# A two-block transformer kernel: seven more constant products at the start, and a final norm that is split over three engines and written out in four transfers

## The reference

```
proj = h @ w_in                       # first product: h is the input with the meta tokens
...
x = x + 0.5 * g3[:, None, :] * swiglu(h, w_gate, w_up, w_down)     # last down-projection
y = x * rsqrt(mean(x * x, axis=-1, keepdims=True) + 1e-6)          # final RMS norm
out = y * final_norm                                               # one weight per channel
```

## Time and profile before

| what | before |
|---|---|
| median of 3 runs | 1286.96 us (1286.91 to 1288.22) |
| profiled execution, its own time | 1286.66 us |
| its span, first to last instruction | 1284.7 us |
| TensorE busy | 1255.6 us, 98% |
| VectorE busy | 994.9 us, 77% |
| ScalarE busy | 685.4 us, 53% |
| GpSimd busy | 54.7 us, 4% |
| DMA, mean over the span | 191 GB/s |
| last chain by engine | TensorE 79%, VectorE 3%, ScalarE 1% |

### The profile page before, as it was taken

How to read it: one execution, slowest core, us unless ns; L and a number is a source line. 1 busy time by engine, 2 the same in 40 slices (tenths; PEclk the granted TensorE clock), 3 DMA queues, 4 the chain that set the end, 5 groups by cost and what they waited for, 6 DMA issues and landing times.

```text
span 1284.7 us, 29083 instructions
## 1 busy us (share of the span) xinstructions
PE 1255.6 (98%) x10579; PEld 1208.9 (94%) x10579; DVE 994.9 (77%) x1818; ACT 685.4 (53%) x1117; POOL 54.7 (4%) x93
## 2 busy tenths in 40 slices
PE   9999999999999999999999999999999999999997
PEld 8998898999999999999998899998899999999986
DVE  6897749998878898998877787775566768877654
ACT  6866445655543544665554565554365566655541
POOL 0012000000001000000000000000000000000000
PEclk9999999999999999999999999999999999999999
DMA  7541123688888588388875366665455336666651
GB/s 270 155 125 35 52 83 116 224 292 269 289 284 287 190 301 285 115 309 270 280 249 169 99 204 186 183 199 192 136 173 189 119 112 183 195 180 184 225 179 34
DMA packets 64778, 244.74 MB, mean 191 GB/s; under 512 B 7200, under 2 KB 8512, under 8 KB 64704
## 3 DMA queue, kind: packets, MB, share of 16 engines
q1 hardware_dynamic: 54048, 204.77, 48.8%
q0 software_dynamic: 10656, 38.93, 9.7%
HBM read 242.63 MB, written 1.05 MB: 190 GB/s over the span
## 4 chain that ended last, share of the span: by engine, by line
PE 79%; DVE 3%; ACT 1%; issue 1%; DVEq 0%; ACTq 0%
PE ps L1805 18%; PE ps L1804 18%; PE ps L1806 18%; PE ps L2170 10%; PE ps L2171 5%; PE ps L1819 1%; PE ps L1825 1%; PE ps L1820 1%; PE ps L2315 1%; PE ps L2317 1%; PE ps L2316 1%; DVE wlo L415 1%; PE ps L2426 1%; PE ps L2220 0%; DVE xb L1447 0%
## 5 line engine op out<-in xcount | busy, mean ns | idle before, releaser
L1804 PE MATMUL ps<-hhi,whi 128*128 128x258 f32 (+4 forms) x1952 | 557.4, 286 | 2.7 <-DVE hlo L1052 1.6
L408 ACT ACTIVATE whi<-raw 128x1024 fp32r<-128x1024 f32 (+1 forms) x360 | 400.3, 1113 | 292.7 <-PE ps L1806 169.9
L1805 PE MATMUL ps<-hlo,whi 128*128 128x258 f32 (+4 forms) x1952 | 555.5, 285 | 0.0
L1806 PE MATMUL ps<-hhi,wlo 128*128 128x258 f32 (+4 forms) x1952 | 550.1, 282 | 0.0
L415 DVE TENSOR_TENSOR wlo<-raw,whi 128x1024 fp32r<-128x1024 f32 (+1 forms) x360 | 463.5, 1293 | 86.4 <-ACT whi L408 81.8
L1804 PEld LDWEIGHTS ps<-hhi,whi 128*128 128x128 f32 x1952 | 369.9, 190 | 5.2 <-DVE wlo L415 4.2
L1806 PEld LDWEIGHTS ps<-hhi,wlo 128*128 128x128 f32 x1952 | 371.3, 190 | 0.0
L1805 PEld LDWEIGHTS ps<-hlo,whi 128*128 128x128 f32 x1952 | 369.9, 189 | 0.3
L2170 PE MATMUL ps<-aboth,whi 128*128 128x512 f32 x528 | 185.3, 395 | 0.0
L2171 PE MATMUL ps<-aboth,wlo 128*128 128x256 f32 x528 | 147.9, 280 | 0.0
L2170 PEld LDWEIGHTS ps<-aboth,whi 128*128 128x128 f32 x528 | 99.1, 188 | 22.9
(11 more groups left out here) (419 smaller groups left out, 1554.0 us busy)
## 6 DMA issues: line engine op xcount, KB each, us to landing
raw<-in_w_up SPq DMA_DIRECT2D x176, 512.0 KB, 4.1
raw<-in_w_down SPq DMA_DIRECT2D x64, 704.0 KB, 4.2
ring<-in_ada_w POOLq DMA_DIRECT2D x72, 512.0 KB, 5.0
raw<-in_w_mix SPq DMA_DIRECT2D x48, 512.0 KB, 3.5
raw<-in_w_a_in SPq DMA_DIRECT2D x32, 512.0 KB, 3.6
raw<-in_w_b_cx SPq DMA_DIRECT2D x16, 512.0 KB, 4.9
raw<-in_w_a_out SPq DMA_DIRECT2D x8, 512.0 KB, 3.6
raw<-in_w_b_gate SPq DMA_DIRECT2D x8, 512.0 KB, 4.4
```

The costliest lines, as they stand in the source:

```text
L408: nc.scalar.activation(whi[:, s, 0:blocks * P], raw[:, s, 0:blocks * P], ACT.Copy).then_inc(hi_split, 1)
L1804: nc.tensor.matmul(out, whi[:, s, w], rhi(k0 + k), start=first and k == 0, stop=False)
L1805: nc.tensor.matmul(out, whi[:, s, w], rlo(k0 + k), start=False, stop=False)
L1806: ins = nc.tensor.matmul(out, wlo[:, s, w], rhi(k0 + k), start=False, stop=last and k == blocks - 1)
```

## The change

Two things, in two places.

1. `WARM_UP` goes from 10 to 17: seven more products of the zeroed tile before the first unit.
2. The last norm. In `down3` ScalarE, after the square of tile m, multiplies `hf[:, m]` in place by the tile's column of weights. VectorE's products then need no column and are 512 wide (two tiles of `hf` by the row, which is read twice with a stride of zero); it makes three of them, tiles 0 to 5. TensorE writes the row a second time, to bank 6; ScalarE copies it to `tb`; GpSimd multiplies tiles 6 and 7 by that copy. SP writes out pairs of tiles, 256 KB each, in the order 0, 2, 6, 4.

```
-WARM_UP = 10
+WARM_UP = 17
...
-            for m in range(KT):
-                sp.wait_ge(y_ready, Y_AT[7] + m + 1)
-                sp.dma_start(io["out"][:, m, :], outb[:, m, :]).then_inc(out_done, 16)
-            sp.wait_ge(out_done, 16 * KT)
+            for i, m in enumerate((0, 2, 6, 4)):
+                if m == 6:
+                    sp.wait_ge(pool_out, 1)
+                else:
+                    sp.wait_ge(y_ready, Y_AT[7] + m // 2 + 1)
+                sp.dma_start(io["out"][:, m:m + 2, :], outb[:, m:m + 2, :]).then_inc(out_done, 16)
+            sp.wait_ge(out_done, 16 * (KT // 2))
...
+            pool.wait_ge(hg_ready, KT)
+            pool.wait_ge(row_copied, 1)
+            nc.gpsimd.tensor_tensor(outb[:, 6:8, :], hf[:, 6:8, 0:SEQ], bcast(tb[:, 0, 0:SEQ], 2), ALU.mult).then_inc(pool_out, 1)
...
                         nc.scalar.activation(sqb[:, m, 0:SEQ], hf[:, m, 0:SEQ], ACT.Square).then_inc(sq_ready, 1)
+                        if name == "down3":
+                            nc.scalar.activation(hf[:, m, 0:SEQ], hf[:, m, 0:SEQ], ACT.Copy, scale=col(m + (V_NORM + 3 * KT))).then_inc(hg_ready, 1)
...
             act_norm(7, SEQ, RMS_EPS, None)
+            act.wait_ge(pool_row, 1)
+            nc.scalar.activation(tb[:, 0, 0:SEQ], ps[6][:, 0:SEQ], ACT.Copy).then_inc(row_copied, 1)
...
                 y_ = ps[7][:, 0:n]
+                if dst is outb:
+                    dve.wait_ge(hg_ready, KT)
+                    for m in range(0, 6, 2):
+                        nc.vector.tensor_tensor(dst[:, m:m + 2, :], src[:, m:m + 2, 0:n], bcast(y_, 2), ALU.mult).then_inc(y_ready, 1)
+                    return
...
                 row(7, SC_RSTD, n, rstd_col, {5: 5, 7: 6}[i]).then_inc(rstd_row, 1)
+                if i == 7:
+                    row(6, SC_RSTD, n, rstd_col, 6).then_inc(pool_row, 1)
                 keep_busy(IDLE_PRODUCTS[i][1])
```

More of the change, by code:

```diff
@@ L312, in build @@
         warm_ready = sem("warm_ready")
+        hg_ready, pool_row, row_copied, pool_out = sem("hg_ready"), sem("pool_row"), sem("row_copied"), sem("pool_out")
         c_ready, b_tap, lo_added = sem("c_ready"), sem("b_tap"), sem("lo_added")
@@ L1787, in _ @@
             down_squares("down3", 8, 7)
-            dve_norm(7, SEQ, hf, NORM_EPS, lambda m: col(V_NORM + 3 * KT + m), None, dst=outb)
+            dve_norm(7, SEQ, hf, NORM_EPS, None, None, dst=outb)
         @block.tensor
```

## The result

The change made the kernel slower: 1289.34 us (22 runs, 1288.36 to 1291.36) against 1287.39 us for the kernel before on the same chip (22 runs, 1286.30 to 1288.54). The ratio is 1.0016, with a 95% interval of 1.0010 to 1.0022. That is 1.3 to 2.8 us; the middle of it lies under the 0.2% that I had called no change. The median lies outside my range by 1.6 us; the forecast was 0.9 us faster. Some 0.4 us of the distance are the kernel before itself, whose median over 22 runs is that much above the one over three. A ratio here is worked out from the runs and is not the quotient of the two medians, so the two differ a little.

A forecast was written before the change was run, and what follows sets the result against it. TensorE bounds the middle (79% of the chain), untouched by the change; SP's issue pace bounds the end. Start 0 and end -0.8 us take the median from 1286.96 to 1286.1, range 1284.7 to 1287.7.

The forecast's parts named there:

- The last lands 2.0 us after its start: End of the kernel before: SP's last transfer lands about 1284.3 and the span ends 0.4 us later.
- GpSimd's product: Last norm, tiles 6 and 7: takes 1.28 us, starts 0.09 after the copy, ends at 1280.50.
- nothing is queued behind either: Last norm: TensorE's second row and ScalarE's copy, ending 1279.13, hold up no later work; first row not delayed.
- The transfers: End, SP's queue: four 256 KB transfers instead of eight, last start 1.30 us earlier, gain taken as 0.8 us.
- Rival D: End: DMA engines keep 270 GB/s whatever SP does, data until 1283.9, median 1287.0 to 1287.2; chance 0.10.
- Rival B: End: GpSimd's product takes 2.3 us beside VectorE and holds the end, median 1287.1 to 1287.2; chance 0.08.
- Rival C: End: GpSimd's product starts late after its long rest, each us adding one to the forecast; chance 0.02.
- The start: First 12 us: seven more products, first unit likely 0.6 to 1.4 us ahead, but 0 kept at the end.
- the cover that was named: TensorE's waits at 22 and 68 us absorb a lead; the 0.8 us at 68 also covers a delay.
- the wait at 68 us: TensorE's wait for ScalarE's last square grows from 0.8 to about 1.1 us or more.
- The scaling in `down3`: Eight ScalarE instructions of 0.495 us, the eighth ending 1276.80 before the root at 1277.10: cost 0, 0.3 us to spare.
- my sign of 0.3 at 70 us: The forecast is wrong if dates at 70 us have moved by more than 0.3 us.

The follow-up runs named there:

- e2: The changed kernel with WARM_UP back at 10: 1289.35 us against 1288.02 for the kernel before, ratio 1.0009.
- e3: The changed kernel without GpSimd, second row or copy at the end; VectorE makes a fourth wide product, WARM_UP 17: 1286.81 us against 1288.02 for the kernel before.
- e5: The VectorE-only end of e3 with WARM_UP back at 10: 1286.46 us against 1287.25 for the kernel before, ratio 0.9993.
- e6: e5 with tiles 6 and 7 as two products and two 128 KB transfers: 1286.02 us against 1287.25 for the kernel before, ratio 0.9988.
- e7: e3 with eight transfers of 128 KB: 1288.00 us against 1287.25 for the kernel before, ratio 1.0002.
- e9: The kernel before with tile 7's transfer issued from GpSimd's queue instead of SP's: 1292.10 us against 1287.35, ratio 1.0033.
- e10: The kernel before with WARM_UP 40: 1289.43 us against 1287.35, ratio 1.0014.
- e4: The kernel before plus a one-column GpSimd memset nobody waits for, released with the row: 1287.90 us against 1288.02, ratio 1.0002.
- e8: e4 with the memset released earlier, by the sum of tile 6: 1287.76 us against 1287.25 for the kernel before, ratio 1.0000.
- e1: The kernel before with WARM_UP 17 and nothing else: 1287.68 us against 1288.02, ratio 1.0001.

## Why the prediction was wrong, step by step

- **What failed** is "The last lands 2.0 us after its start, about 1284.3, and the span ends 0.4 later", carried over to the changed kernel, where the sum has the last landing at 1283.35 and no term for what follows GpSimd's product. I took the end of the kernel to be the last landing plus 0.4 for any program, and my description of the kernel before says as much ("The kernel ends when all of them have landed"). It is the last of five engines' drains plus some 0.2, and SP's drain stands right behind the landing. The phrase "nothing is queued behind either" was said of TensorE's and ScalarE's new instructions and held for them; what is queued behind the new GpSimd product, the drain of its engine, I put at nothing without asking. The runs showed 6.13 us in its place. Such a drain stood in the trace of before, 7318 ns at 918.5, on a line that I did not open since the page counts no drain as busy.
- The account closes with it. From the row to the end of the span: 6.2 us before, 8.4 after (1278.98 to 1287.4). The change's own share is 2.03 us from row to the end of GpSimd's product, 6.13 of drain, 0.2 to the last semaphore. 2.2 us more in the span, less 0.3 that lie outside it now, is 1.9; measured 1.95 by the medians. These 0.3 the prediction did not have: 1.6 to 1.7 us lie around the span in every run of the kernels with the new norm (after, e2, e3, e5, e6, e7) and 1.9 to 2.0 in those of the others. GpSimd doesn't make them (e3 has them without it), nor the number of transfers (e7), nor the products at the start (e5); what does stays open.
- The transfers: forecast 0.8 earlier. Without GpSimd (e3) the end moved by 0.9 in the trace, from 6.2 to 5.3 us after the row, and the medians by 1.2 (e3) and 0.8 (e5), with the 0.3 outside the span in them. The mechanism was right, and e7 shows it by taking it away. Rival D (the DMA engines keep their 270 GB/s) fell: 387 GB/s with transfers twice the size. The fit that the prediction takes from the Trainium skill stands there for transfers from GpSimd's queue (DMA: Bandwidth & Descriptors, Anatomy of one DMA). By it 128 KB land after 2.3 us, as e9's transfer from that queue did; SP's landed after 2.0 us, and those of 256 KB after 2.2 where the fit gives 2.6.
- GpSimd's product: 1.28 forecast, 1.26 measured, beside three VectorE products. Rival B fell, and the Trainium skill's rule on the shared interface agrees (GPSIMD Engine Reference, Specifications; 1.26 us here). Rival C fell as well: 0.14 us from the copy's end at 1279.60 to the product's start, after 360 us of rest. The prediction had 6 us more in rival C, with 0.02, but ahead of the product. That a time of this size stood behind it is no merit of the forecast, and no run shows that the two have anything to do with each other.
- The Trainium skill (VectorE: DVE Perf Modes, The DRAIN you can't avoid) describes the drains that the runtime puts before and after a program as some 12 ns on all five engines. The drains here stand at the close of the program's own block, so they need not be the same, and the figure doesn't carry over to them: SP's took 7 ns, GpSimd's 6232 to 7421 ns.
- The start: worth nothing, as forecast, by the cover that was named. One detail was wrong. I expected the wait at 68 us to grow from 0.8 to 1.1; it stayed 0.8, and the whole lead went into the wait for abm at 22 us (1.1), which itself was ready 0.5 us later than before (22.27 against 21.76). The cover against a delay was somewhat larger than the 0.8 I gave: 1.1 in the trace of e10.
- The scaling in `down3` cost nothing: it ends at 1277.22, the root starts at 1277.62.
- The 0.5 us of later dates in the profiled execution went over my sign of 0.3 at 70 us, but it follows the weights' date: e2, with ten products, got its weights at 16.72 and reached the products at 68 us at 68.67, as late as the changed kernel's 68.69.
- The range was too narrow on the slow side for a reason: all its cases were of what I had added to the path that I saw, none of what an engine does when the program is over.

## What to carry to other kernels

Before giving an engine work near the end, look at its drain on the closing line of the trace, and add it to the engine's last instruction: here nothing of GpSimd's, neither a product nor the issue of a transfer, should start within about 7 us of the end. Count the issues at the end rather than the bytes: half as many transfers, each twice the size, were the whole gain that this change had between the row and the end. And before paying for a faster start, look for the next date that comes from elsewhere.

## What the runs showed of the hardware

- GpSimd's closing drain lasted 6.1 to 6.2 us beyond its last instruction where that stood near the end: 6.1 behind a memset of 0.10 us (e4, e8) and behind the product of 1.26 (after, e2), 6.2 behind a DMA issue of 0.55 (e9). Where its last instruction was the issue of the load of `dft` at 918 to 921 us, the drain lasted 7104 to 7318 ns, which is 6.6 to 6.8 beyond the issue (seven traces). What it does in that time no run shows. The ends of GpSimd's instructions are rough in a profile, so these remainders are less sure than the drains themselves.
- TensorE's level at the start differs between executions of the same products. With ten, the first real products ran at 0.227 us spacing in the profiled execution of before and in e5, at 0.125 us in e4 and e8; e2, e6 and e9 began at 0.125 and fell back to 0.227 from about 8.4 to 11.7 us. With seventeen it was 0.125 in all four traces, which is too few to call the products the cause. None of it reached the products at 68 us, which followed the weights in all eleven traces.
- TensorE's level just before the row differs between executions too, and the times counted from the row leave it out. After the sums TensorE has 0.94 us without work, then makes the row's two products. They took 0.43 us at a granted clock of 1.00 (before, e1, e9, e10), and 0.69 where it had fallen to 0.50 (e3, e5 to e8): the row came 0.25 us later.
- A transfer of 256 KB to memory landed 2.2 us after its issue began, one of 128 KB 2.0 us. SP's issue was as long for either size. What made it longer was that it followed another at once: 0.45 us then (the median of the eight of before, and the last of the four of the changed kernel), and 0.33 to 0.35 after a pause.
